# A decoder layer in one core: both SwiGLU down projections as seven block products, with resident weights and stored sums of activations

## What is computed

```python
def swiglu(h, w_gate, w_up, w_down):
    return (jax.nn.silu(h @ w_gate) * (h @ w_up)) @ w_down

# D_MODEL = 1024, SEQ = 1024, D_FF = 2816, all f32
h = modulate(rms_norm(x, g_ffn1[l]), sh1, sc1)
x = x + 0.5 * ga1[:, None, :] * swiglu(h, w_gate1[l], w_up1[l], w_down1[l])
h = modulate(rms_norm(x, g_mix[l]), sh2, sc2)
y = hybrid_mixer(h, positions, w_in[l], ...)
x = x + ga2[:, None, :] * y
h = modulate(rms_norm(x, g_ffn2[l]), sh3, sc3)
x = x + 0.5 * ga3[:, None, :] * swiglu(h, w_gate2[l], w_up2[l], w_down2[l])
return rms_norm(x, g_final)
```

## Time and profile before

| | us |
|---|---|
| median of three runs | 2383.17 |
| lowest and highest | 2382.65, 2384.37 |
| profiled execution, its own time | 2382.41 |
| span in that profile (first to last instruction) | 2380.6 |
| PE busy in the span | 2299.2 (97%) |
| DVE, ACT, POOL busy | 1410.8, 1089.1, 1255.5 |
| granted TensorE clock, mean | 0.989 |

### The profile page before, as it was taken

One profiled execution on the slowest core, in us unless ns is written; L12 is line 12 of the kernel. 1 busy time (PEld: TensorE's weight loads), 2 busy tenths in 40 slices (PEclk: granted clock), 3 DMA queues, 4 the chain that ended last, 5 costly groups with the idle time before them and its releaser, 6 DMA issues. The chain is left out here.

```text
span 2380.6 us, 30086 instructions
## 1 busy us (share of the span) xinstructions
PE 2299.2 (97%) x10920; PEld 1874.9 (79%) x10920; DVE 1410.8 (59%) x1668; ACT 1089.1 (46%) x2060; POOL 1255.5 (53%) x963
## 2 busy tenths in 40 slices
PE   4999999999999999999999999999999999999997
PEld 2878888888888788888777877788778888888885
DVE  4855555347666746742788888568872333324544
ACT  3533333333444554344788888425643333333332
POOL 3454444445665566454557555356754555544463
PEclk7999999999999999999999999999999999999998
DMA  6155454255542343353814046324222222255362
GB/s 252 43 208 190 181 189 148 85 207 173 163 154 99 98 151 129 148 186 119 227 53 108 15 107 171 111 89 151 98 89 71 89 79 81 89 180 173 115 189 85
DMA packets 128946, 314.98 MB, mean 132 GB/s; under 512 B 13408, under 2 KB 34016, under 8 KB 128800
## 3 DMA queue, kind: packets, MB, share of 16 engines
q1 hardware_dynamic: 127824, 310.76, 39.0%
q10 hardware_dynamic: 976, 2.29, 0.4%
HBM read 241.51 MB, written 69.34 MB: 131 GB/s over the span
## 5 line engine op out<-in xcount | busy, mean ns | idle before, releaser
L1686 POOL TENSOR_TENSOR r_z<-f_main,r_z 128x512 fp32r<-128x512 f32 x254 | 357.3, 1411 | 394.5 <-ACT r_z L1069 394.5
L2639 PE MATMUL ps<-r_main,r_z 128*128 128x512 f32 x1232 | 482.8, 392 | 12.6 <-issue 7.1
L2641 PE MATMUL ps<-r_main,r_z 128*128 128x512 f32 x1232 | 480.4, 390 | 0.0
L2640 PE MATMUL ps<-r_main,r_z 128*128 128x512 f32 x1232 | 480.3, 390 | 0.0
L1692 POOL TENSOR_TENSOR r_main<-f_main,r_main 128x1024 fp32r<-128x1024 f32 x88 | 219.0, 2492 | 213.5 <-ACT r_main L1112 213.4
L2639 PEld LDWEIGHTS ps<-r_main,r_z 128*128 128x128 f32 x1232 | 231.8, 188 | 64.4 <-issue 9.6
L2641 PEld LDWEIGHTS ps<-r_main,r_z 128*128 128x128 f32 x1232 | 231.8, 188 | 48.5
L2640 PEld LDWEIGHTS ps<-r_main,r_z 128*128 128x128 f32 x1232 | 231.9, 188 | 48.1 <-issue 0.2
L2615 PE MATMUL ps<-r_main 128*128 128x512 f32 x688 | 268.7, 391 | 0.0
L1069 ACT CAST r_z<-f_main 128x512 fp32r<-128x512 f32 x254 | 155.6, 619 | 245.3 <-PE ps L2641 212.9
L2617 PE MATMUL ps<-r_main 128*128 128x512 f32 x688 | 267.8, 389 | 0.0
(11 more groups left out here) (325 smaller groups left out, 4629.5 us busy)
## 6 DMA issues: line engine op xcount, KB each, us to landing
f_main<-in_wd SPq DMA_DIRECT2D x88, 512.0 KB, 3.6
f_main<-in_w_ada SPq DMA_DIRECT2D x56, 512.0 KB, 5.0
act_d<-f_main SPq DMA_DIRECT2D x88, 256.0 KB, 2.0
f_main<-act_d SPq DMA_DIRECT2D x88, 256.0 KB, 3.7
f_main<-in_wg SPq DMA_DIRECT2D x20, 1024.0 KB, 4.9
f_main<-in_wu SPq DMA_DIRECT2D x20, 1024.0 KB, 5.0
f_main<-in_wmix SPq DMA_DIRECT2D x18, 1024.0 KB, 5.6
r_main<-qk_hi_d SPq DMA_DIRECT2D x40, 256.0 KB, 7.5
```

The source lines that it names most:

```text
L1686: pool.tensor_tensor(prod_lo_t[slot], source_of(g), prod_hi_t[slot].bitcast(F32), ALU.subtract).then_inc(s["wl"], 1)
L2639: pe.matmul(out, wh, hi, start=start, stop=False, skip_group_check=True)
L2640: pe.matmul(out, wh, lo, start=False, stop=False, skip_group_check=True)
L2641: return pe.matmul(out, wl, hi, start=False, stop=stop, skip_group_check=True)
```

## The change

**The product.** With the two tiles of a pair and the two halves of the output features the weights of a pair are four quadrants, and with the two halves of the tokens so are the activations and the output. The down projection becomes seven block products in Winograd's form, in the order q = 1, 7, 6, 2, 4, 5, 3, each over 11 pairs j: 77 steps g. A step has four output tiles m of three matmuls, 12 matmuls. Accumulators move on from one product to the next inside PSUM: product 7's bank is copied by ACT (`down_seed`, two copies for each m), DVE adds in `down_u3` and `down_c22`. The last two pairs of each product are run one m at a time, so that the m's finish one after another.

**Weights.** All four quadrants of all 11 pairs stay in SBUF (`d_quad`), loaded once for each feed-forward in pieces of up to 1 MB. Their sums, 44 DVE instructions of 128x512 for each feed-forward, are made in place (`down_sum`), at most two in a step, at steps that `D_SUMS_AT` sets. Casts and lows of the weights are now 128x512 and one a step. The rings of high and low parts have three slots each, of 128x512 (before four, the weights' 128x1024); the raw activations have four.

**Activations.** `act_sums`, new on DVE, makes four differences of a pair's quarters after each pair, 128x512 each. SP stores three of the quarters and these four, seven blocks for each pair (before four quarters), in `b_d`, and a step loads the one block that it needs.

**Other work moves.** rope_tables stands in steps 6 to 18, the Sins at 16 and 22. The eight loads of x, before all at the start of the down projection, stand in steps 25 to 32. The squares and the normalized x of the first half come in steps of products 5 and 3. GATES and VC are loaded at step 24, and GATES is cast after the last step, in front of KC and VC; SP's wait for the lows of GATES in front of KC's load is as before.

```diff
+D_ORDER = (1, 7, 6, 2, 4, 5, 3)
+D_STEPS = [(q, j) for q in D_ORDER for j in range(PAIRS)]
+D_WRING, D_BRING, D_RAW = 3, 3, 4
+for j in range(PAIRS):
+    for n, g in ((3, D_AT[7, j] - 1), (1, D_AT[7, 5 + j] - 1 if j < 6 else D_AT[6, j - 6] - 1), (2, D_AT[6, j] - 1), (4, D_AT[5, j])):
+        D_SUMS_AT.setdefault(g, []).append((n, j))
+D_EARLY = {D_AT[3, 0] + 5 * m // 4: m for m in range(NT)}
...
             def down_loads(f, k, stores=False):
...
+                for q in range(4):
+                    sp.wait_ge(s["st"][q], z["st"] + 16 * PAIRS)
+                sp.wait_ge(s["tst"], z["tst"] + 48 * PAIRS)
+                for g in range(D_RAW, D_N):
+                    down_rows(f, g)
...
+                    if 25 <= g < 25 + NT:
+                        n = (4, 5, 6, 7, 0, 1, 2, 3)[g - 25]
+                        sp.dma_start(x[:, n, :], aps["xT"][n] if f == 0 else x_d[n]).then_inc(s["xin"], 16)
...
             sp.wait_ge(both["wl"], mb["wl"] + 2)
             sp.dma_start(plain_raw[KC_T], aps["wmix"][KC_T]).then_inc(m_["raw0"], 16)
...
             def plain_high(e):
                 if e == GATES_T:
+                    act.wait_ge(both["dn"], D_PHASE * len(D_ORDER))
                     act.wait_ge(m_["raw0"], 16)
...
             def mix_high():
+                plain_high(GATES_T)
                 plain_high(KC_T)
                 plain_high(VC_T)
...
             def mix_low():
+                plain_low(GATES_T)
                 plain_low(KC_T)
                 plain_low(VC_T)
...
+                dve.wait_ge(nsem["hl"], HL[k] + 4 * len(X_ORDER))
+                act_sums(f, 0)
...
+            def act_sums(f, p):
+                dve.wait_ge(s["act"], z["act"] + 4 * (p + 1))
...
+                dve.tensor_tensor(act_t[0], act_q[1], act_q[0], ALU.subtract).then_inc(s["ts"], 1)
+                dve.tensor_tensor(act_t[2], act_q[3], act_q[1], ALU.subtract).then_inc(s["ts"], 1)
+                dve.wait_ge(s["ts"], at + 1)
+                dve.tensor_tensor(act_t[1], act_q[3], act_t[0], ALU.subtract).then_inc(s["ts"], 1)
+                dve.wait_ge(s["ts"], at + 3)
+                dve.tensor_tensor(act_t[3], act_q[2], act_t[1], ALU.subtract).then_inc(s["ts"], 1)
             def gate_up(f):
                 for g in range(PRELUDE, N_PROD):
                     if g > PRELUDE and g - 1 != AT[1, GATE, 6]:
                         taken(f, g - 1)
+                    if g > PRELUDE and PRODUCTS[g - 1][1:] == (UP, 3):
+                        act_sums(f, PRODUCTS[g - 1][0])
                     p, b, q = PRODUCTS[g]
                     if f == 0 and 3 <= p <= 9 and (b, q) == (GATE, 1):
                         mod(p - 1, ps_mod)
...
-                for t in range(4, 2 * NF):
-                    down_low(f, t)
-                    if f == 0 and 4 <= t <= 16:
+                for g in range(3, D_N):
+                    for e in D_SUMS_AT.get(g, ()):
+                        down_sum(f, *e)
+                    down_low(f, g)
+                    if f == 0 and 6 <= g <= 18:
...
                         for _ in range(2):
                             next(tables, None)
...
+                def step(g, m):
+                    if m == 0:
+                        pe.wait_ge(s["wl"], z["wl"] + N_PROD + g + 1)
+                        pe.wait_ge(s["dbl"], z["dbl"] + g + 1)
...
+                    wh, wl = (w[g % D_WRING][:, m * P:(m + 1) * P] for w in (d_wh, d_wl))
+                    mm = product3(bank, wh, wl, d_bh[g % D_BRING], d_bl[g % D_BRING], q in (1, 7) and j == 0, j == PAIRS - 1)
```

More of the change, by code:

```diff
@@ L387, in build @@
         ps_mod = ps[:, 2, 0:NT]
-        stat_of = [[ps_at(4 if k in (1, 3) and h == 0 else 6 + h) for h in range(NH)] for k in range(4)]
+        stat_of = [[ps_at(h if k in (1, 3) else 6 + h) for h in range(NH)] for k in range(4)]
         rope_s, rope_c = ft(13), ft(12)
-        ang, turns, part_f = ft(15), ft(16), ft(18)
+        ang, turns, part_f = ft(10), ft(16), ft(18)
         plain_raw = [ft(11), ft(11), ft(10)]
@@ L733, in gate_up_loads @@
                         act_store(f, p, i)
[L734 to L742 removed]
+                    for i in range(4):
+                        act_sum_store(f, p, i)
             def down_loads(f, k, stores=False):
@@ L756, in down_loads @@
                         for n in range(NT):
-                            sp.wait_ge(s["x"], z["x"] + n + 1)
                             sp.dma_start(x_d[n, :, halves(0)], x[:, n, halves(0)]).then_inc(s_spill[0], 16)
-                    if f == 0 and t == 4:
-                        sp.wait_ge(s["mm"], z["mm"] + N_PROD)
-                        sp.dma_start(part_f.bitcast(I32), aps["pos"].partition_broadcast(P)).then_inc(q_["pos"], 16)
-                    if stores and NF + 9 <= t < NF + 9 + NT:
-                        output(t - NF - 9)
+                if stores:
+                    for m in range(NT):
+                        output(m)
@@ new lines, in down_u3, with down_c22 @@
+            def down_u3(f, m):
+                s, z = fsem[f], fbase[f]
+                dve.wait_ge(s["dn"], z["dn"] + d_part(6, m))
+                dve.wait_ge(s["p7"], z["p7"] + D_U + m + 1)
+                dve.wait_ge(s["x"], z["x"] + D_ADD_AT[4 + m, 0])
+                dve.tensor_tensor(d_a[m], d_b[m], d_p7[m], ALU.add).then_inc(s["u3"], 1)
+            def down_c22(f, m):
+                s, z = fsem[f], fbase[f]
+                dve.wait_ge(s["dn"], z["dn"] + d_part(5, m))
+                dve.wait_ge(s["u3"], z["u3"] + D_U + m + 1)
+                dve.tensor_tensor(d_p7[m], d_b[m], d_p7[m], ALU.add).then_inc(s["c22"], 1)
@@ L2613, in product3 @@
             def product3(out, w, wl, m, ml, start, stop):
-                pe.matmul(out, w, m, start=start, stop=False)
-                pe.matmul(out, w, ml, start=False, stop=False)
-                return pe.matmul(out, wl, m, start=False, stop=stop)
+                pe.matmul(out, w, m, start=start, stop=False, skip_group_check=True)
+                pe.matmul(out, w, ml, start=False, stop=False, skip_group_check=True)
+                return pe.matmul(out, wl, m, start=False, stop=stop, skip_group_check=True)
             def mod_mm(out, total, ready=None):
@@ L2731, in mix_plain @@
+                for q in D_ORDER:
+                    for j in range(PAIRS - D_LAST):
+                        for m in range(D_UNITS):
+                            step(D_AT[q, j], m)
+                        if (q, j) == (5, 6):
+                            pe.wait_ge(s["x"], z["x"] + NT)
+                            stat(norm, 0)
+                    for m in range(D_UNITS):
+                        for j in range(PAIRS - D_LAST, PAIRS):
+                            step(D_AT[q, j], m)
             def mix_plain():
```

387 lines of the change are left out of this document (250 added, 137 removed).

## The result

| | before | after |
|---|---|---|
| median | 2383.26 us | 2432.46 us |
| lowest, highest | 2382.65, 2384.37 | 2428.81, 2435.94 |
| span of the profiled execution | 2380.6 us | 2427.1 us |
| PE busy in it | 2299.2 us | 2272.4 us |
| mean granted clock | 0.989 | 0.979 |

The ratio is 1.0206, with an interval from 1.0194 to 1.0218: about 2% slower. The forecast was 2391, with a range to 2411. The direction was right and the size was not: the span grew by 46.5 us where the sum said 7.8. The profiled execution is the fastest of the four.

A forecast was written before the change was run, and what follows sets the result against it. The prediction took the down projections to be bound by the number of matmuls. Saving 59.9 us against added waits summed to +7.8 us, giving a median of 2391.0 us, own range 2379 to 2402, 8-in-10 range 2366 to 2411.

The forecast's parts named there:

- Matmuls, -59.9: Both down projections: 264 fewer matmuls at 0.2267 us each, paying in full while feeders keep up, -59.9 us.
- First pair, +5.4: After each feed-forward's first pair: four uncovered DVE differences take about 2.7 us, twice, +5.4 us.
- rival D: Mainly down 1's steps 6 to 18: PE falls to the 1.2 GHz clock behind waits, +20 us, 2411; chance 0.14.
- Later pairs, +14.7: Starts of pairs 3 to 9: differences ahead of `mods` make PE wait 2.0 to 2.1 us seven times, +14.7 us.
- Tables, +16.0: Down 1, steps 6 to 17: rotary tables, lows and weight sums overfill DVE, 48.6 us against PE's 32.6, +16.0 us.
- The rest of down 1, +10.0: Down 1 outside the tables: first loads, steps 19 to 25, ACT copies, seams and the last product, +10.0 us.
- down 2, +4.0: Second down projection: start 0.7, weight sums 1.0, seams 0.8, last product 1.5, together +4.0 us, from 0 to 9.
- The prediction's own rule: Where DVE and POOL meet: a POOL instruction of 1.29 us costs a busy DVE 1.1 us.
- The seam, +17.6: From down 1 to the mixer: GATES' casts and KC's late load delay the squares; PE waits 13 us, +17.6 us.
- B: Whole kernel: DVE and POOL hardly meet, feeders keep pace, only uncovered waits remain, -26 us, 2357; chance 0.13.
- C: Down 1: rotary tables mostly hidden, its two terms shrink from 26 to 8 us; -14.9 in all, 2368; chance 0.17.
- E: Both down projections: activation loads share the weights' queues and come 7 us late in each, +14 us, 2405; chance 0.14.

## Why the prediction was wrong

**Matmuls, -59.9: right.** Product 2 of both projections ran with no overrun, 132 matmuls in 29.92 us, 0.2267 each.

**First pair, +5.4: right as a wait.** The waits grew from 1.37 to 4.08 us and from 1.48 to 4.18. The clock behind them, which the prediction kept in rival D, added 1.2 and 2.0 us.

**Later pairs, +14.7: right as a wait, and short in two terms.** Seven waits of 1.98 us idle, 2.13 from pace to pace, make 14.9. Not in the sum: a wait of 1.2 us for u3 in pair 1 (at 160.88), and four falls of the clock of 1.5 us. This stage was forecast at 17.4 us and cost 28.1, and the kernel before with the differences alone showed all of it. The POOL instruction met a difference and made it 1.77 us long, as in the earlier trace rows:

```profile
233.76 1.77 DVE L2172 TENSOR_TENSOR f_main<-f_main 128x512 f32<-128x512 f32 x1
235.46 0.68 DVE L2174 TENSOR_TENSOR f_main<-f_main 128x512 f32<-128x512 f32 x1
236.17 0.69 DVE L2176 TENSOR_TENSOR f_main<-f_main 128x512 f32<-128x512 f32 x1
236.78 0.16 DVE L2114 TENSOR_TENSOR mods<-ps,b_ada_sb 128x8 f32<-128x8 f32 x1
```

**Tables, +16.0: right.** 14.7 by the run that moved them. The price of a POOL low to a busy DVE, from the earlier trace rows, held.

**"The rest of down 1, +10.0" and "down 2, +4.0": the step that failed, with the clock below.** The seven overruns of down 1 make 41.6 us, those of down 2 17.7. The kernel before ran 1.7 us over in each, and the tables are 14.7 in down 1. So 25.2 us are left where the term had 10.0, and 16.0 where it had 4.0. The largest piece is product 5, 9.0 and 7.4 us, or 7.7 and 6.1 without the matmuls of the sum of squares. The prediction priced its steps nowhere: it spoke of the steps with three DVE instructions at 19 to 25, of seams, and of product 3. Yet the change puts into product 5 at once a weight sum in each step, four additions of x, eight squares, six sums of them, the root and the reciprocal. All but the weight sums stood before in steps of 5.44 us, and they moved to steps of 2.72 us. The prediction's own rule would have priced the full steps: two DVE instructions and two of POOL are 2 x 0.61 + 2 x 1.1 = 3.4 us, and 3.40 was measured. The second piece is product 3, 7.4 and 3.0 us where it had 4 and 1.5. Its price of 4.1 us for a full step was right, for in down 1 PE's waits at 754.14, 758.22 and 762.21 are 4.08 and 3.99 apart; what was wrong is how much of it the ring and idle steps would catch up. The third is product 7's end, 3 us in both. There PE goes through the last two pairs one output tile at a time, so it needs the lows of both at once, and that was in the text of the change. That weight sums, casts and lows form a cycle was seen only when one of them was moved.

**The seam, +17.6: right.** +19.5 measured, of which 12.35 us are the idle time that was forecast at 13. Of it the load made 4.3 us and the order 4.9.

**The clock: the mechanism was a rival, D, at 0.14, and it came true at another place.** It was to decide in the table stretch, +12.8 us there. There only two waits, at 559 and 584 us, were followed by five or more matmuls at 0.43 us, but over the whole kernel matmuls at the lower clock added 14.9 us. They should have been a term of the sum: the prediction made nine waits of 2 us and more in the first two terms alone, and it had read that after one of 2.07 us eight matmuls took 0.43 us each. (Six did, between one of 0.59 us and one of 0.29; the 1.6 us that it gave for all eight are right.) If half of them fell, that would have been 9 x 1.6 x a half, an estimated 7 us.

So 38.7 us of the span were missed: 14.9 in the clock and most of the rest, about 21, in places of the down projections that were not counted or counted too low, of which product 5 is the largest. Where a wait was worked out instruction by instruction, it held to 2 us; where a place got a discount (product 3) or "1.0" or "0.8" for seams, it did not.

**The rivals.** B and C (fast feeders, hidden tables) fell. E fell too: a block's load landed 2.6 us after its issue in the median, where one of before took 3.7, and no wait of PE was ended by a load in the down projections.

## What to carry to other kernels

Fewer matmuls of the same size shorten every step, and all that stood in a step stays: make a table of each step's work for each engine, at the new length, for all steps, and not for the crowded ones that come to mind. A small instruction on an engine that is 60% busy is free only where nobody waits for what stands behind it; the later pairs' differences cost 23 us at one place and nothing that shows 10 us later. When PE begins to wait in many places, price each wait with what the clock does behind it.

## What the runs showed of the hardware

The fourteen traces hold 577 waits of PE of half a microsecond or more in the feed-forwards and the mixer's start, measured from pace to pace, most of them the same places in kernel after kernel. Waits in front of the sums of squares are left out. What the next matmuls did, up to the next wait:

| wait, us | count | followed by four or more matmuls at 0.43 us | mean loss in matmuls of 0.35 to 0.53 us, us |
|---|---|---|---|
| 0.5 to 2.05 | 415 | 2 | 0.0 |
| 2.05 to 2.8 | 109 | 54 | 0.9 |
| 2.8 to 3.6 | 35 | 29 | 1.3 |
| over 3.6 | 18 | 18 | 1.9 |

The groups are those of these kernels, and few places fill the upper three. Waits of the same length at the same place fell in one execution and not in another: of 49 waits of 2.12 to 2.15 us, 29 fell. That is one source of the spread in the times. The changed kernel's four executions lie 7 us apart (2428.8 to 2435.9), the kernel before's within 2.

A DVE instruction that met a POOL instruction took about 1 us longer: 0.68 became 1.77 us at 233.76, and 0.69 became 1.66 at 585.49, where POOL's own time is 1.29. No run here took POOL's work away, so how much of the down projections' overrun this makes was not measured by itself.
